# Second network of a fused block: a softmax shift taken as the minimum of negated scores, and the low rows of each finished pair of heads written one step later

## The reference, cut to what matters

```python
bias = rel_bias_table[t5_bucket(rel)]
logits = jnp.where(valid, logits + bias, -jnp.inf)
m = jnp.maximum(jnp.max(logits, axis=-1, keepdims=True), sink)
p = jnp.exp(logits - m)
p = p / (jnp.sum(p, axis=-1, keepdims=True) + jnp.exp(sink - m))
out = jnp.einsum('bnkgqs,bnskd->bnqkgd', p, vb)
```

```python
s = (einsum(qn, k_nope) + einsum(qr, k_rope)) * scale
s = jnp.where(key_pos <= q_pos, s, -jnp.inf)
p = jax.nn.softmax(s, axis=-1)
out = einsum('bhqs,bshd->bqhd', p, v)
```

## Time and profile before

| what | value |
|---|---|
| median of three runs | 1324.12 us (1323.63 to 1324.32) |
| the profiled execution | 1324.01 us, its span 1321.5 us |
| PE busy | 1268.9 us, 96% of the span |
| DVE busy | 899.6 us, 68% |
| ACT busy | 666.4 us, 50% |
| POOL busy | 245.5 us, 19% |
| mean granted clock of TensorE | 0.993 |

### The profile page before, as it was taken

One profiled execution on the slowest core, in us unless ns is written; L12 is line 12 of the kernel. 1 busy time (PEld: TensorE's weight loads), 2 busy tenths in 40 slices (PEclk: granted clock), 3 DMA queues, 4 the chain that ended last, 5 costly groups with the idle time before them and its releaser, 6 DMA issues.

```text
span 1321.5 us, 26629 instructions
## 1 busy us (share of the span) xinstructions
PE 1268.9 (96%) x10035; PEld 1137.7 (86%) x10035; DVE 899.6 (68%) x1764; ACT 666.4 (50%) x1276; POOL 245.5 (19%) x376
## 2 busy tenths in 40 slices
PE   6999999989889999999999998999999999999997
PEld 5889999888889997999988987888888977888886
DVE  5678888756755576788846566777745775877744
ACT  4355555544246645666635356544434576544332
POOL 0001322121444421232302000112200000122200
PEclk9999999999999999999999999999999999999999
DMA  7322211114411144545555522455554632455552
GB/s 322 117 77 72 92 65 66 66 65 152 168 65 65 65 158 161 189 171 181 191 192 191 185 90 97 160 190 186 179 199 167 200 120 96 152 182 180 187 193 93
DMA packets 26772, 189.89 MB, mean 144 GB/s; under 512 B 2961, under 2 KB 3089, under 8 KB 4401
## 3 DMA queue, kind: packets, MB, share of 16 engines
q1 hardware_dynamic: 25632, 182.55, 38.3%
q0 software_dynamic: 1040, 5.96, 1.5%
HBM read 186.40 MB, written 1.05 MB: 142 GB/s over the span
## 4 chain that ended last, share of the span: by engine, by line
PE 80%; DVE 7%; ACT 5%; DMA 2%; DVEq 2%; issue 1%; POOLq 1%; SPq 0%; ACTq 0%; POOL 0%
PE ps L604 32%; PE ps L665 12%; PE ps L552 12%; PE ps L667 6%; PE ps L913 3%; DMA ring<-in_weights 2%; DVE ring_r L2054 2%; PE ps L577 1%; ACT early_r L1409 1%; DVE w_lo L2067 1%; PE ps L758 1%; PE ps L584 1%; PE ps L930 1%; PE ps L576 1%; PE ps L1004 1%
## 5 line engine op out<-in xcount | busy, mean ns | idle before, releaser
L1510 ACT ACTIVATE w_hi<-ring 128x1024 fp32r<-128x1024 f32 x125 | 132.6, 1060 | 296.0 <-PE ps L604 156.9
L2067 DVE TENSOR_TENSOR w_lo<-ring,w_hi 128x1024 fp32r<-128x1024 f32 x125 | 155.4, 1243 | 128.0 <-ACT w_hi L1510 127.8
L665 PE MATMUL ps<-h_both,w_hi 128*128 128x512 f32 x672 | 237.7, 399 | 0.0
L667 PE MATMUL ps<-h_both,w_lo 128*128 128x256 f32 x672 | 189.1, 281 | 0.0
L604 PE MATMUL ps<-h_both,w_hi 128*128 128x256 f32 x912 | 165.7, 285 | 0.8 <-DVE w_lo L2073 0.8
L2073 DVE TENSOR_TENSOR w_lo<-ring,w_hi 128x1024 fp32r<-128x1024 f32 x125 | 157.4, 1259 | 0.0
L665 PEld LDWEIGHTS ps<-h_both,w_hi 128*128 128x128 f32 x672 | 126.4, 188 | 31.2
L552 PE MATMUL ps<-oT_r,ring_r 128*128 128x256 f32 x512 | 145.9, 285 | 0.0
L604 PEld LDWEIGHTS ps<-h_both,w_hi 128*128 128x128 f32 x912 | 142.6, 192 | 1.4 <-DVE w_lo L2073 1.1
L1515 ACT ACTIVATE w_hi<-ring 128x1024 fp32r<-128x1024 f32 x125 | 130.8, 1046 | 0.0
L604 PE MATMUL ps<-h_both,w_lo 128*128 128x256 f32 x456 | 129.2, 283 | 0.0
(11 more groups left out here) (446 smaller groups left out, 2966.7 us busy)
## 6 DMA issues: line engine op xcount, KB each, us to landing
ring<-in_weights SPq DMA_DIRECT2D x170, 1024.0 KB, 4.8
arena<-in_aux POOLq DMA_DIRECT2D x1, 2112.0 KB, 12.7
grow<-in_rows POOLq DMA_DIRECT2D x3, 512.0 KB, 4.1
cst<-in_consts SPq DMA_DIRECT2D x1, 1497.5 KB, 14.6
x<-in_x SPq DMA_DIRECT2D x1, 1024.0 KB, 5.0
arena<-in_swbias POOLq DMA_DIRECT2D x1, 1024.0 KB, 9.9
arena<-arena POOLq DMA_DIRECT2D x1, 1024.0 KB, 9.0
out<-xn SPq DMA_DIRECT2D x4, 256.0 KB, 2.3
```

The costliest lines, as they stand in the source:

```text
L665: pe.matmul(bank[:].rearrange("p (a t) -> p a t", a=2), hi, h_both[:, :, k, :], start=k == 0, stop=False)
L667: m = pe.matmul(bank[:, 0:S], lo, h_hi[:, k, :], start=False, stop=k == KT - 1)
L1510: act.activation(w_hi[:, half_of(u0, m), WH:], ring[:, (u0 + m) % RING, WH:], ACT.Copy).then_inc(w_hi_p, 1)
L2067: dve.tensor_tensor(w_lo[:, half_of(u0, m), WH:], ring[:, (u0 + m) % RING, WH:], w_hi[:, half_of(u0, m), WH:].bitcast(F32), ALU.subtract). ...
```

## The change

`softmax_max` no longer takes a maximum and negates it. The scores are produced negated (the factor in the queries is -SCALE and -MLA_SCALE, the masks and the window table have the opposite sign), the custom instruction adds and keeps the minimum, and this goes straight to the columns that ACT reads as bias; the sink enters as a minimum with its negative. ACT's exponentials get `scale=-1.0`. The negated sinks are made once by DVE (128 x 8), the negated window table by four POOL instructions of 128 x 512 behind the wait for its transfer, ahead of the barrier; DVE waits for those at step 8.

`out_low` of pair p moves from step 2p + 4 to step 2p + 5 for p = 0 to 5 and stays in steps 16 and 18 for p = 6 and 7 (`low_due`). In each step it now stands ahead of `take_pT` and of the two L2609 queries, where before it stood behind them. Both loops have this.

```diff
 def softmax_exp(t, j, sink=None):
     act.wait_ge(a_max, t + 1)
-    act.activation(..., ACT.Exp, bias=am[:, j, 2:3],
+    act.activation(..., ACT.Exp, bias=am[:, j, 2:3], scale=-1.0,
...
 def softmax_max(j, bank, first_bias, second_bias, sink=None):
     for a, b, bias in ((0, P, first_bias), (P, KEYS, second_bias)):
-        dve.tensor_tensor_reduce(out=probs[j][:, a:b], in0=bank[:, a:b], in1=bias, scale=1.0,
-                                 scalar=-3e38, op0=ALU.add, op1=ALU.max,
-                                 accum_out=am[:, j, a // P:a // P + 1])
-    dve.drain()
+        m = dve.tensor_tensor_reduce(out=probs[j][:, a:b], in0=bank[:, a:b], in1=bias, scale=1.0,
+                                     scalar=3e38, op0=ALU.add, op1=ALU.min,
+                                     accum_out=am[:, j, 2 + a // P:3 + a // P])
     if sink is not None:
-        dve.tensor_scalar(am[:, j, 0:2], am[:, j, 0:2], sink, None, ALU.max)
         dve.drain()
-    dve.tensor_scalar(am[:, j, 2:4], am[:, j, 0:2], -1.0, None, ALU.mult).then_inc(a_max, 1)
+        m = dve.tensor_scalar(am[:, j, 2:4], am[:, j, 2:4], sink, None, ALU.min)
+    m.then_inc(a_max, 1)
...
+def low_due(s):
+    return [p for p in range(H // 2) if s == (2 * p + 4 if 2 * p + 5 >= H else 2 * p + 5)]
...
 # layer 0, DVE, for s in range(H + 3):
+    for p in low_due(s):
+        out_low(p)
     if SB_HEADS + 2 <= s < H + 2:
         take_pT(s - 2, s % 2)
     if s in (3, 4):
         take_even_query(s - 3)
-    if s >= 3 and s % 2 == 0:
-        out_low((s - 4) // 2)
     out_weights(U["even_out"], "even_out", s, 3, (6, 8))
...
 # MLA, DVE, for s in range(H + 3):
     if s in (3, 5):
         take_queries(6 + s // 5, 6 + s // 5)
+    for p in low_due(s):
+        out_low(KT + p)
     if 2 <= s < H + 2:
         take_pT(H + s - 2, s % 2)
-    if s >= 3 and s % 2 == 0:
-        out_low(KT + (s - 4) // 2)
...
 # POOL, before the barrier:
+pool.wait_ge(swb_in, 16)
+for h in range(0, SW_HEADS, 2):
+    m = pool.tensor_scalar(swb[:, h:h + 2, :], swb[:, h:h + 2, :], -1.0, None, ALU.mult)
+m.then_inc(root_ready, 1)
```

More of the change, by code:

```diff
@@ L1525, in softmax_exp @@
                 act.wait_ge(a_max, t + 1)
-                act.activation(probs[j][:, 0:P], probs[j][:, 0:P], ACT.Exp, bias=am[:, j, 2:3],
+                act.activation(probs[j][:, 0:P], probs[j][:, 0:P], ACT.Exp, bias=am[:, j, 2:3], scale=-1.0,
                                accum_out=am[:, j, 4:5])
-                m = act.activation(probs[j][:, P:KEYS], probs[j][:, P:KEYS], ACT.Exp, bias=am[:, j, 3:4],
+                m = act.activation(probs[j][:, P:KEYS], probs[j][:, P:KEYS], ACT.Exp, bias=am[:, j, 3:4], scale=-1.0,
                                    accum_out=am[:, j, 5:6])
@@ L2609, in take_even_query @@
                 dve.scalar_tensor_tensor(qbP[:, 2 * n:2 * n + 2, :], ps[6 + n][:].rearrange("p (a t) -> p a t", a=2),
-                                         SCALE, of_keys, ALU.mult, ALU.mult).then_inc(e_hi, 1)
+                                         -SCALE, of_keys, ALU.mult, ALU.mult).then_inc(e_hi, 1)
+            minus_sinks = mx2[:, 0, :]
+            dve.tensor_scalar(minus_sinks, small("sinks"), -1.0, None, ALU.mult)
             for b in range(2):
@@ L2630, in _ @@
                     if h == 0:
-                        dve.wait_ge(swb_in, 16)
+                        dve.wait_ge(root_ready, 3)
                     if h < 3:
@@ L2634, in _ @@
                     dve.wait_ge(a_scores, s + 1)
-                    softmax_max(s % 3, ps[s % 2], swb[:, h, P:S], swb[:, h, :], sink=small("sinks")[:, h:h + 1])
+                    softmax_max(s % 3, ps[s % 2], swb[:, h, P:S], swb[:, h, :], sink=minus_sinks[:, h:h + 1])
                 if SB_HEADS < s <= H:
                     softmax_sum(s - 1 - SB_HEADS, (s - 1) % 3, sink=True)
+                for p in low_due(s):
+                    out_low(p)
                 if SB_HEADS + 2 <= s < H + 2:
@@ L2692, in _ @@
             dve.drain()
-            dve.tensor_scalar(rope_q, rope_t, MLA_SCALE, None, ALU.mult)
+            dve.tensor_scalar(rope_q, rope_t, -MLA_SCALE, None, ALU.mult)
             dve.drain()
-            dve.memset(rope_q[0:HD], MLA_SCALE)
+            dve.memset(rope_q[0:HD], -MLA_SCALE)
             low_rank_part(2, 1, 0)
@@ L2985, in _constants @@
     put("dist", np.where(rel >= 0, rel, BIG))
-    put("causal", np.where(rel >= 0, 0.0, -BIG))
+    put("causal", np.where(rel >= 0, 0.0, BIG))
     put("strict", np.where(rel > 0, 0.0, -BIG))
```

## The result

Measured: 1332.24 us, median of four runs (1331.71 to 1333.23), against 1324.22 of the kernel before in the same comparison. The ratio is 1.0061, interval [1.0046, 1.0077]: 8.0 us slower. The forecast was 1327.6 with a range to 1331.5. The sign was right; the time lies just outside the range, and the loss of 8.0 us is more than twice the forecast +3.5.

The account below looks back on a forecast made before the run. PE, 96% busy, was the bound, leaving 4.25 us winnable in layer 0 and 1.36 in MLA. Layer 0 +3.1 and MLA +0.4 gave +3.5 on 1324.01, 1327.5, or 1327.6 as median; range 1324.8 to 1331.5.

Parts of the forecast that it names:

- rival A: Layer 0: PE's new 4.8 us gap before values(2) halves the clock, values(3) about 3.2 us later, 1330.8; chance 0.25.
- part 1: Layer 0, steps 4 to 7: later low rows leave PE idle 4.8 us before values(2), make values(4) 6.04 us late.
- Part 2: Layer 0, steps 8 to 18: old stalls vanish -4.25 us, odd-step waits +0.6, `out_low(6)` ahead of step 16's copy +0.7.
- Part 3: Softmax minimum: exponentials 0.25 to 0.3 us earlier; MLA gains 0.3, its step-16 copy comes 0.43 later; MLA +0.4 us.
- Part 4: Before the barrier: POOL's four table negations, 4 to 6 us, are hidden; the small sink operation falls in DVE idle time.
- B: Both loops: low rows of pairs 0 and 1 ready in time, gain shows without loss, 1319 to 1320; chance 0.1.
- C: Layer 0's loop costs its 6 us, but the later steps' new waits don't come: 1325 to 1326.5; chance 0.15.
- D: Softmax: the minimum form saves nothing (column as late as 1.22 us), 0.3 per step in eight steps: 1330; chance 0.05.

Follow-up runs that it names:

- E4: The changed kernel, order untouched, with extra unread PE products filling the idle gaps ahead of values(2) and values(4) in layer 0: 1326.61 us, ratio 1.0025.
- E7: The changed kernel with `out_low(6)` put behind `take_pT` in step 16 of both loops: 1328.09 us, ratio 1.0036.
- E8: The changed kernel with layer 0's pairs 0 and 1 at steps 4 and 6, other low rows up to pair 6 heading step 2p + 5: 1317.95 us.
- E2: The kernel before with the new steps and places of the low rows in both loops, maximum and negation as before: 1330.11 us, ratio 1.0055.
- E3: The changed kernel with the low rows of pairs 0 and 1 of layer 0 back in steps 4 and 6: 1318.74 us, ratio 0.9970.
- E6: The changed kernel with 28 extra unread PE products ahead of values(2) alone, filling only the first gap: 1327.94 us, ratio 1.0040.
- E1: The changed kernel with the low rows at their old steps and places in both loops, leaving the minimum form alone: 1320.84 us, ratio 0.9975.
- E5: The changed kernel with the low rows of pair 0 alone of layer 0 back in step 4: 1324.96 us, ratio 1.0016.

## Why the prediction was wrong, step by step

**The step that failed** is the choice against rival A, and it rests on one sentence: "Against it: all gaps seen were harmless", with its row. The row is true and the sentence isn't. It took the clock behind the longest gap for the clock behind all. The window 378 to 383 of the kernel before has a clock of 0.66: half clock from 378.81, 1.4 us behind the end of an idle gap of 2.06 us at 377.43. The window 1044 to 1048 has 0.57, there with no longer gap ahead of it than 0.60 us, behind twenty products of two columns (L1335, 2.29 us). Both stood in the granted clock of the trace of before. With them the evidence for A was: half clock can follow a gap less than half as long as the new one. A had deserved most of the chance, with 1330.8. So the sum has no term for the clock, and this term measured 3.67 us (E4). The prediction's own sign for A, a clock under 1.00 behind 783 us, came.

That the gap of 2.28 us in the earlier trace rows was harmless holds for that one trace: the same gap in the kernel after (287.81, L1014), where nothing was changed, is followed by half clock, 0.50 over 288.50 to 291.80. In the ten traces, one of each kernel, the gap of 2.28 us is followed by half clock in six, that of 2.06 in two, those of 2.74 and 2.75 in four of five, and that of 4.83 in all three; E4 has half clock even behind one of 1.77 us (357.10 to 363.80). So one trace can't show that such a gap is harmless.

**The whole difference.** The spans differ by 8.7 us where 3.5 was forecast. The missing 5.2 are 3.67 of clock in layer 0's loop, 0.65 of order there (3.75 for 3.1), 0.06 in MLA's loop, and 0.8 outside the loops.

By the Trainium skill (TensorE: Matmul & The Clock Gate, "Why this matters for your kernels") an idle gap over some 3 us between bursts sends the clock to half. For the gap of 4.83 us the trace agrees (0.50 over the 6.8 us from 780.00 to 786.80). For 2.75, 2.28 and 2.06 us, which lie under the Trainium skill's figure, half clock followed as well, though not each time; the measurement decides.

A itself was under-sized. It counted one drop, and 3.2 us (and took 6.4 us for the early stretch at half clock, which runs from 27.2 to 34.1, 6.8 us). Two came, since the second gap, which part 1 had (2.9 forecast, 2.75 measured), was as much a gap as the first. Together they cost 3.67 (E4): values(3) is 5.22 us later than before at the half clock and 3.1 at full clock, so the first costs 2.1, and the rest, 1.6, belongs to the second. That A's 3.2 comes near 3.67 is luck: it was half as much again as the one drop that it counted, since 2.5 of the 6.8 us of half clock passed while PE stood idle, and it left the other drop out.

**Part 1** was right: gap 4.83 (forecast 4.8), values(2) 3.89 late (3.88). For values(4) the working was for full clock, so E4 is its test: 34.18 us after the loop's start against 28.27, **5.91 late** (6.04).

**Part 2** had two terms too small and lacked a third. At full clock the loop was to lose 3.1 and lost 3.75. From values(4) on PE won 5.91 - 3.75 = 2.16 us back, where -4.25 + 0.6 + 0.7 = -2.95 was forecast. Behind the second gap the first odd step is 3.34 us, and then the steps alternate between 3.11 and 3.23, where the undisturbed step of before is 3.03. So the odd ones lose 0.3 once and then 0.20 (I had 0.15 in each of the four), and the even ones 0.08, which the sum hadn't counted. Except for 0.14 in the first, none of it shows as idle time, only as distance from one start to the next. The starts around two value products of the kernel after show where both lie:

```profile
814.58 0.67 PE L758 MATMUL ps<-pT,arena 128*128 128x256 f32 x2
815.09 0.38 PE L759 MATMUL ps<-pT,arena 128*128 128x128 f32 x2
...
817.69 0.59 PE L758 MATMUL ps<-pT,arena 128*128 128x256 f32 x2
818.12 0.38 PE L759 MATMUL ps<-pT,arena 128*128 128x128 f32 x2
```

values(10) at 814.58, which waits, starts 0.43 us after the product ahead of it, values(11) at 817.69 0.23 after: this is the 0.20. From L758 to L759 it is 0.51 us behind the wait and 0.43 without one: this is the 0.08, the longer form behind a wait that part 1 had at 0.07 and part 2 left out. In step 13 the operation behind the sink's stands 0.86 us after the custom instruction, where I had 0.78; that is enough for what the wait has over 0.15. The step with `out_low(6)` cost 0.97 (E7) where I had 0.7. 0.3 for the odd steps, 0.3 for the even ones and 0.3 for `out_low(6)` are about the 0.8 us missing.

**Part 3** was right. MLA's loop grew by 0.46 (forecast +0.4). Its two terms are seen apart in E7: with the copy ahead of `out_low(6)` the loop is 0.37 shorter than before (I had 0.3), and the place of `out_low(6)` takes 0.83 (I had 0.31 + 0.43 = 0.74). The exponential comes 0.68 us after the custom instruction in most heads of MLA, and 0.99 in six of the eight of layer 0, as forecast (1.35 and 1.41 in the other two):

```profile
1075.65 0.29 DVE L2097 CUSTOM_DVE_ANT_0 sc<-ps,cst 128x128 f32<-128x128 f32 x1 [0.48 <-PE ps L1380]
...
1076.33 0.40 ACT L1526 ACTIVATE sc<-sc,am 128x128 f32<-128x128 f32 x1 [1.69 <-DVE am L2097]
```

**Part 4** was right: the four operations end 22.6 us ahead of the barrier at 757.57, and the loop's start is no later than before.

```profile
729.02 5.96 POOL L2949 TENSOR_SCALAR arena<-arena 128x512 f32<-128x512 f32 x4 [5.17 <-DMA arena<-in_swbias]
```

**Rivals B, C, D.** B is out (its wait came), D too (0.68). C is out: the odd-step waits came. But B's sum was sound as a bound: with pairs 0 and 1 in time, E8 gets 3.1 of the 4.25 in layer 0 and 0.84 of 1.36 in MLA.

**What was outside the loops.** +1.15 us lie between them, where nothing was changed. There the stretch at half clock ahead of MLA is longer: 6.8 us after, 3.4 before. The ten traces account for all of it. Between the loops the three without half clock (E2, E3, E6) take 234.7 us, the five with 3.4 us of it (before, E1, E4, E5, E7) 236.2, and the two with 6.8 us (after, E8) 237.4. Such stretches come and go with the execution. The kernel before has, in 20 runs on one chip, a mean clock of 0.997 at 1321.76 us and of 0.992 at 1324.75; behind the gap of 2.06 us at 377.43 the clock falls in the traces of before and E7 and in none of the others. E3's profiled execution has a span 6.1 us below before's with 1.8 of it in the loops; outside them it has 3.4 us at half clock where before has 13.7, leaving out the end of the program. That E3's runs have a median clock of 0.997, and those of before 0.993, fits its 5.1 us in the median. Why the clock falls outside the loops in one kernel more often than in another stays open; so of E3's and E8's 5.1 us only 1.8 and 3.95 are explained by the loops.

## What to carry to other kernels

Before an operation is moved later, find which buffer it frees and follow who waits for that buffer back to the operation itself: here the low rows free the bank of the value product that feeds the chain ahead of the low rows, and 6 us of latency went around a loop with 3.2 us of work in it. A new idle gap on TensorE is to be priced twice, as idle time and as a stretch at half clock behind it: here half clock followed every gap of 4.83 us and some of the shorter ones, down to 1.77. The granted clock of the whole span is to be read for that first, and of more than one execution. Waiting of an engine that isn't the bound (DVE's 22.2 us) is no gain to be had: the 11.1 us saved there came with a loss at the end.

## What the runs showed of the hardware

- Half clock doesn't begin or end with the gap: it lasted 6.8 us from inside a gap of 4.83 us, 3.4 us from inside one of 2.75 (both after), 3.4 us from 1.4 us behind one of 2.74 (E5), and once it didn't come after 2.75 (E6). What it costs is half of the part that falls on work: 7.4 of 10.2 us, for 3.67.
- A gap in the part that all ten kernels share is followed by half clock in one trace and not in the next: that of 2.28 us in six of ten, that of 2.06 us in two. What decides wasn't found.
- Half clock also came without a gap over 0.6 us: in seven of the ten traces ahead of MLA's loop, during or up to 1.7 us behind twenty products of two columns (L1335 in before).
- Filling the two gaps with products that nobody reads kept the clock at 1.00 and won 3.67 us of the loop, at no cost to the work behind it: values(4) starts 34.18 us after the loop's start with both gaps filled (E4), 34.26 with one (E6).
- A short wait needn't show as idle time, as the ends of the products are modelled: values(10) comes 0.20 us late with no gap in its row. And from the start of L758 to that of L759 it is 0.51 us behind a wait, instead of 0.43.
